# One diffusion block on one core: the loads of the beginning in another order, 1.4 MB of them cut or put off, c turned with the filter's vectors, the latents scaled by two engines, and context's tokens turned later

## The chip, the core and the metric

The kernel runs on one core of a Trainium2 chip, with these engines: TensorE (matrix products and transposes, into eight banks of PSUM), VectorE, ScalarE, GpSimd and SyncE, which here only issues loads. ScalarE and GpSimd issue loads too. Weights lie in HBM. The metric is the device time of one execution in microseconds (us); lower is better. All times in this text are microseconds unless they say otherwise, and "at 52.10" means 52.10 us after the start of the profiled span.

## The reference, cut to what matters

One block works on 512 latent tokens `x` and 256 context tokens `ctx` of width 1024 in float32. The beginning, which the change touches, is:

```python
x = x + pos_embed_2d(rows, cols, D)                   # half of the width by row, half by column
mod   = silu(c)     @ w_mod + b_mod                   # shifts, scales, gates for latents
mod_c = silu(c_ctx) @ w_mod + b_mod                   # the same for context
h  = rmsnorm(x,  pre_norm1) * (1 + sc1)  + sh1
hc = rmsnorm(xc, pre_norm1) * (1 + csc1) + csh1
z  = h @ w_in                                         # 3088 columns
zc = hc @ w_in[:, HY_COLS:]                           # context: only the mLSTM columns, gates among them
# the hyena filter: a small network of positions, times a decay
h = sin(freq * (zf @ w1 + b1)); h = sin(freq * (h @ w2 + b2)); h = sin(freq * (h @ w3 + b3))
filter = (h @ w4) * exp(-t * abs(deltas))             # then its spectrum
```

Behind it come the long convolution (by spectra), the mLSTM in both directions, the output projection, a router, and 16 experts of three matrices of 8 MB each, 404 MB in all, each used once. The last part is most of the time.

## The kernel before

All is written out by hand: each engine runs its own list, and the lists meet in semaphores (`wait_ge` on one side, `then_inc` on the other). A load increments its semaphore by 16 when it has landed. SyncE issues nearly all loads, in the order written, and its loads land in about that order.

**Weights.** A ring of eight slots of 2 MB takes the tiles of `LOADS`: four tiles of w_mod, here m0 to m3 (`mod_tile(0)` to `mod_tile(3)` use them), then six of w_in, i0 to i5, two of w_out, then the experts'. m0 and m2 share slot 0, m1 and m3 slot 1, i0 slot 0 again; a tile that reuses a slot is issued once the products of the tile before it there are done (`S["p_w"]`). The other two thirds of w_mod, in sixteen parts of 1 MB, are multiplied by the vector on VectorE (`row_parts`), between its convolutions (`conv`).

**The beginning, engine by engine.** TensorE turns the small vectors (L569 and L586 to L588), runs the filter's three layers (L582), each waiting for the sine before it, makes eight taps of the filter (L597), which VectorE multiplies by the decays `dcy` (L1533), and then `mod_tile(0)` and `mod_tile(1)` (L616), spectra 0 to 2 of the filter (L665), `mod_tile(2)`, spectrum 3, `mod_tile(3)`. The products with w_mod take silu(c) and silu(c_ctx) as `cpad`. ScalarE makes the decays (L1252), the sines (L1255), copies the first half of each spectrum (L1263), and squares the six tiles of tokens, context's two first (L1275); the square root of the sums (L1287) follows. VectorE adds the positions to x (L1551), makes parts of each spectrum (L1557, L1558), and after the reciprocal (L1566) normalizes context's and the latents' tiles (L1571); it copies the rows of w_mod's products to `mrow` (L1581).

**Turning.** TensorE turns `mrow` (`mod_turn`, L636), from which VectorE works out scale and shift (`aff1`, six small operations), and turns the normalized tokens, one k of eight at a time, latents and context in turn (L696). ScalarE scales and shifts the eight of the latents (L1293) and VectorE the eight of context (L1618), into `ht`. Then come the gates (L706), for all tokens, and tile 0 of w_in (`hyena_tile(0)`, L716): four groups m of eight products, 6.9 us each.

```python
            pe.wait_ge(S["a_htl"], KD)
            pe.wait_ge(S["v_htc"], KD)
            pe.wait_ge(d_gate, 32)
```

Of the kernel before, what the change touches and what calls it, by code (L numbers as in the profile page):

```python
# [51 lines left out]


def shape_constants():
# [17 lines left out]
    def emb(n):  # L72
# [4 lines left out]
    pe = np.concatenate([np.broadcast_to(er[:, None, :], (rows, GRID_W, D // 2)),  # L77
                         np.broadcast_to(ec[None, :, :], (rows, GRID_W, D // 2))], axis=-1)
    pe = np.ascontiguousarray(pe.reshape(L, D).astype(np.float32))
# [8 lines left out]
    dl = np.ascontiguousarray(np.broadcast_to(deltas[None, :], (P, HY)).astype(np.float32))  # L88
# [11 lines left out]
    return {"cst": cst, "pos": pe, "zft": zft, "dl": dl, "dft": tiles(fwd), "idft": tiles(inv)}  # L100
# [14 lines left out]
def block_kernel(nc, A, out):  # L115
    ctx = ExitStack()
    with ctx:
# [241 lines left out]
        def _(sp):  # L359

            def rows(dst, r, src, n):
                sp.dma_start(dst[r:r + n, :], src.rearrange("(a b) -> a b", b=P)).then_inc(d_vec2, 16)
# [133 lines left out]
        def _(pool):  # L496
            g = nc.gpsimd
            g.memset(vr2, 0.0).then_inc(S["g_ms"], 1)
# [4 lines left out]
            for r, n, src in ((R_C, 8, A["c"][0]), (R_CC, 8, A["c_ctx"]), (R_PRE1, 8, A["pre_norm1"][0]),  # L503
# [49 lines left out]
        def _(pe):  # L553
# [13 lines left out]
            pe.wait_ge(d_cst, 32)  # L567
            pe.wait_ge(d_vec2, 16 * N_VEC2)
            tr(B[1][:, 0:R2_ROWS], vr2[0:R2_ROWS, :], upper(R2_ROWS)).then_inc(S["p_vt"], 1)  # L569

            for n in range(3):
                if n < 2:
                    pe.wait_ge(*((d_filt, 32), (d_fw, 64))[n])
                if n:
                    pe.wait_ge(S["a_fil"], n)
                for half in range(2):
                    r = slice(FH * half, FH * (half + 1))
                    if n == 0:
                        w, src = fw1[0:FEMB, :], zft[0:FEMB, half * LC:(half + 1) * LC]
                    else:  # L580
                        w, src = (fw2, fw3)[n - 1][r, :], fh[r, :]
                    x = mm(B[2][r, (n % 2) * LC:(n % 2 + 1) * LC], w, src, start=True, stop=True)  # L582
                x.then_inc(S["p_fil"], 1)
                if n == 0:
                    pe.wait_ge(d_vec1, 16 * N_VEC1)
                    tr(B[0][:, 0:R1_ROWS], vr1[0:R1_ROWS, :], upper(R1_ROWS))  # L586
                    tr(B[0][:, 128:140], vr3[0:12, 0:2 * P:2], upper(12))
                    tr(B[0][:, 140:152], vr3[0:12, 1:2 * P:2], upper(12)).then_inc(S["p_vt"], 1)  # L588
            users[0] = users[1] = (S["v_vt"], 2)
            pe.wait_ge(S["v_fws"], 2)  # L590
            pe.wait_ge(S["a_fil"], 3)
            for n, (w, c) in enumerate(TAPS):
                b = 4 + n % 4
                r = slice(FH * (c // 2), FH * (c // 2 + 1))
                if n >= 4:
                    pe.wait_ge(S["v_kf"], n - 3)
                mm(B[b][:, :], fh[r, (c % 2) * P:(c % 2 + 1) * P], fws[r, w, :], start=True, stop=True)\  # L597
                    .then_inc(S["p_kf"], 1)
                users[b] = (S["v_kf"], n + 1)
# [8 lines left out]
            def mod_tile(i):  # L608
# [3 lines left out]
                if kp == 0:  # L612
                    take(2)
# [1496 lines left out]
```

## Time and profile before

| what | value |
|---|---|
| median of three runs | 1329.31 (1327.12 to 1329.52) |
| the profiled execution | 1328.1, span 1326.1 |
| TensorE busy | 1206.1 (91%) |
| VectorE, ScalarE, GpSimd busy | 351.3 (26%), 187.8 (14%), 30.6 (2%) |
| moved from HBM | 453 MB, mean 343 GB/s over the span |
| granted clock of TensorE | 0.996 of full speed |

The profiled execution's time is 2.0 more than its span: what lies around the span. Busy shares are means over the whole; the stages differ, so the page is read by stretches, and the waits by what ended last.

### The profile page before, as it was taken

How to read it: one execution, taken by the hardware profiler on the slowest of the kernel's cores; microseconds unless marked ns; L12 is line 12 of the kernel's file. 1: busy time of each engine (PE TensorE's matmuls, PEld its weight loads, DVE VectorE, ACT ScalarE, POOL GpSimd, SP SyncE). 2: the span in 40 equal slices, each digit the busy share in tenths (PEclk: the TensorE clock that was granted, in tenths of full speed). 3: DMA queues.
4: the chain of work that ended last, by engine and by line, in shares of the span. 5: the costliest groups of instructions: out<-in, count | busy, mean ns of one | idle time of the engine just before them, and what ended most of it. 6: DMA issues, size and time to landing. Idle time of an engine off the chain costs nothing.

```text
span 1326.1 us, 12939 instructions
## 1 busy us (share of the span) xinstructions
PE 1206.1 (91%) x5274; PEld 505.1 (38%) x5274; DVE 351.3 (26%) x625; ACT 187.8 (14%) x388; POOL 30.6 (2%) x56
## 2 busy tenths in 40 slices
PE   5999999999999999998989798888979898897996
PEld 1444454554554353342325234232423422242332
DVE  3775739444450110210201111020102102010213
ACT  2510020133310111010101001010200101010012
POOL 2000020000000001000000000000000000000000
PEclk9999999999999999999999999999999999999998
DMA  9965410306168999999999999999999999999994
GB/s 347 400 233 207 143 64 0 128 1 254 66 250 363 415 426 428 427 428 429 428 428 428 429 428 428 428 428 430 428 428 428 428 429 428 429 429 427 428 427 166
DMA packets 44776, 455.55 MB, mean 344 GB/s; under 512 B 6192, under 2 KB 6304, under 8 KB 16970
## 3 DMA queue, kind: packets, MB, share of 16 engines
q1 hardware_dynamic: 44098, 454.94, 82.1%
q8 instruction: 22, 0.36, 0.1%
q10 hardware_dynamic: 264, 0.11, 0.0%
q0 software_dynamic: 384, 0.07, 0.0%
q14 instruction: 8, 0.07, 0.0%
HBM read 453.01 MB, written 2.10 MB: 343 GB/s over the span
## 4 chain that ended last, share of the span: by engine, by line
PE 60%; DMA 33%; DVE 4%; issue 1%; ACT 1%; SPq 1%; DVEq 0%; ACTq 0%
DMA ring<-in_w_exp_up 28%; PE B L1151 15%; PE B L1120 11%; PE B L716 6%; PE B L953 4%; PE B L1062 4%; PE B L837 3%; DMA ring<-in_w_exp_down 3%; PE B L895 2%; DMA ring<-in_pos 2%; PE B L1212 2%; PE B L766 2%; DVE moe L2029 1%; PE B L1133 1%; DVE yacc L2020 1%
## 5 line engine op out<-in xcount | busy, mean ns | idle before, releaser
L1120 PE MATMUL B<-ring,moe 128*64 128x512 f32 x2032 | 454.9, 596 | 75.9 <-DMA ring<-in_w_exp_up 41.9
L1120 PEld LDWEIGHTS B<-ring,moe 128*64 128x64 f32 x2032 | 139.4, 137 | 384.8 <-issue 247.0
L2029 DVE TENSOR_TENSOR moe<-moe,B 64x512 f32<-64x512 f32 x64 | 43.8, 685 | 699.5 <-PE B L1120 698.2
L1151 PE MATMUL B<-ring,moe 128*64 128x512 f32 x1008 | 221.2, 594 | 4.5 <-DMA ring<-in_w_exp_down 4.4
L1151 PEld LDWEIGHTS B<-ring,moe 128*64 128x64 f32 x1008 | 71.2, 137 | 142.8 <-issue 138.0
L1438 ACT ACTIVATE moe<-B 64x512 f32<-64x512 f32 x64 | 37.9, 592 | 413.8 <-PE B L1120 412.6
L716 PE MATMUL B<-ring 128*128 128x512 f32 x192 | 83.6, 594 | 0.0
L1212 PE MATMUL B<-moe 128*128 128x512 f32 x112 | 56.7, 618 | 4.5 <-DVE yacc L2020 4.1
L1062 PE MATMUL B<-moe,xl 128*128 128x128 f32 x448 | 55.0, 281 | 0.0
L1448 ACT ACTIVATE moe<-B 64x512 f32<-64x512 f32 x31 | 18.4, 592 | 251.3 <-PE B L1151 250.9
L1062 PEld LDWEIGHTS B<-moe,xl 128*128 128x128 f32 x448 | 53.9, 196 | 0.0
L716 PEld LDWEIGHTS B<-ring 128*128 128x128 f32 x192 | 36.1, 190 | 45.1 <-issue 45.1
L837 PE MATMUL B<-ring 128*128 128x512 f32 x96 | 43.3, 592 | 0.0
L2020 DVE TENSOR_TENSOR yacc<-yacc,B 128x512 f32<-128x512 f32 x56 | 38.3, 684 | 10.8 <-PE B L1212 10.4
L895 PE MATMUL B<-ring 128*128 128x512 f32 x64 | 33.1, 614 | 0.0
L1212 PEld LDWEIGHTS B<-moe 128*128 128x128 f32 x112 | 18.4, 189 | 37.7 <-DVE yacc L2020 26.8
L953 PE MATMUL B<-ring 128*128 128x512 f32 x64 | 28.5, 592 | 0.0
L953 PE MATMUL B<-ring,fr 128*128 128x512 f32 x64 | 28.3, 595 | 0.0
L766 PE MATMUL B<-ring 128*128 128x512 f32 x64 | 27.9, 594 | 0.0
L837 PEld LDWEIGHTS B<-ring 128*128 128x128 f32 x96 | 17.4, 190 | 17.7 <-issue 17.7
L1133 PEld LDWEIGHTS B<-cst_sb,moe 128*128 128x128 f32 x128 | 18.9, 204 | 11.5 <-issue 8.2
L2033 DVE COPY moe<-B 128x512 f32<-128x512 f32 x16 | 11.1, 692 | 44.2 <-PE B L1133 44.2
(335 smaller groups left out, 800.7 us busy)
## 6 DMA issues: line engine op xcount, KB each, us to landing
ring<-in_w_exp_up SPq DMA_DIRECT2D x64, 2048.0 KB, 31.8
ring<-in_w_exp_gate SPq DMA_DIRECT2D x63, 2048.0 KB, 30.4
ring<-in_w_exp_down SPq DMA_DIRECT2D x63, 2048.0 KB, 34.0
ring<-in_w_in SPq DMA_DIRECT2D x6, 2048.0 KB, 9.0
ring<-in_w_mod SPq DMA_DIRECT2D x10, 1024.0 KB, 7.6
ring<-in_w_mod SPq DMA_DIRECT2D x4, 2048.0 KB, 14.2
fr<-in_w_mod SPq DMA_DIRECT2D x6, 1024.0 KB, 9.3
ring<-in_w_out SPq DMA_DIRECT2D x2, 2048.0 KB, 8.4
```

Source lines behind the costliest of these rows:

```text
L716: x = mm(B[b][:, :], w[:, k, m * P:(m + 1) * P], ht[:, k, LC:], start=(k == 0), stop=(k == KD - 1))
L766: x = mm(B[b][:, :], w[:, k, m * P:(m + 1) * P], ht[:, k, LC:], start=(k == 0), stop=(k == KD - 1))
L837: x = mm(B[b][:, :], ht[:, k, t * P:(t + 1) * P], w[:, k, :], start=(k == 0), stop=(k == KD - 1))
L895: x = mm(B[O_BANK[c]][:, :], ht[:, k, LC + c * P:LC + (c + 1) * P], wo_in[:, k, :], start=(k == 0), stop=(k == KD - 1))
L953: x = mm(B[b][:, :], lhs, wo[half][:, k, :], start=(k == 0), stop=(k == KD - 1))
L1062: x = mm(B[6 + g][:, k * P:(k + 1) * P], x3[:, c, pair_rows(dk)], psel[:, c, :], start=(c == 0), stop=(c == NLT - 1))
L1120: x = mm(B[n][rows, :], xst[:, 2 * q + k, CAP * e2:CAP * (e2 + 1)], w[:, k, n * CH:(n + 1) * CH], start=(q == 0 and k == 0), stop=(q == 3 ...
L1151: x = mm(B[bank][CAP * half:CAP * (half + 1), :], src[:, q // 2, k * P + at:k * P + at + CAP], wd[:, k, half * CH:(half + 1) * CH], start= ...
L1212: mm(B[6 + half][:, :], pwt[:, c, :], ye[:, half * CH:(half + 1) * CH], start=True, stop=True).then_inc(S["p_sca"], 1)
L1438: a.activation(sil[o, n // 2, :], B[n][i, :], ACT.Silu).then_inc(S["a_sil"], 1)
L2020: v.tensor_tensor(dst, dst, B[6 + half][:, :], ALU.add).then_inc(S["v_yacc"], 1)
L2029: v.tensor_tensor(hid[o, n // 2, :], sil[o, n // 2, :], B[n][o, :], ALU.mult).then_inc(S["v_hid"], 1)
```

## The change

- **SyncE's order.** c and c_ctx come first, now with the filter's vectors in `vr2`; then the part of the constants that is needed early (260 of 836 columns), the filter's inputs and weights, m0, x, the positions, the transform `dft`, m1, ctx, m2, m3, then the rest of the constants. conv_w, conv_b and ml_norm go to GpSimd's queue; zft, filt_w1 and filt_w2 go from ScalarE's queue to SyncE's. The wait for a memset of `vr2` is gone with the memset.
- **Fewer bytes.** Instead of a table of 2 MB the positions are `pcol` (128 x 512, added to all four tiles) and `prow` (8 x 512), read by two loads that each repeat rows over 64 partitions. The decay rates come as one row of 2 KB, which TensorE spreads over 128 partitions by a product with ones.
- **c.** silu(c) is now c / (1 + exp(-c)), by one exponential and three small operations of VectorE, between layers 0 and 1 of the filter. The other vectors are turned after the sixth tap.
- **Decays.** ScalarE makes them after the third sine, from PSUM.
- **Tokens.** x is squared and normalized before ctx. TensorE turns three k of the latents, then `mrow`, then the other five; ScalarE scales the even k and VectorE the odd. Context's eight k are turned within tile 0, behind its first group, and the gates are behind its second.

```diff
-            sp.dma_start(cst[:, :], A["cst"]).then_inc(d_cst, 16)
-            sp.dma_start(dlb, A["dl"]).then_inc(d_cst, 16)
-            sp.wait_ge(S["g_ms"], 1)
+            for r, src in ((R_C, A["c"][0]), (R_CC, A["c_ctx"])):
+                sp.dma_start(vr2[r:r + 8, :], src.rearrange("(a b) -> a b", b=P)).then_inc(d_vec2, 16)
+            sp.dma_start(cst[:, 0:C_EARLY], A["cst"][:, 0:C_EARLY]).then_inc(d_cst, 16)
+            sp.dma_start(zft[0:FEMB, :], A["zft"]).then_inc(d_filt, 16)
+            sp.dma_start(fw1[0:FEMB, :], A["filt_w1"][0]).then_inc(d_filt, 16)
+            sp.dma_start(dlr[0:1, :], A["dl"]).then_inc(d_filt, 16)
...
             for n in range(len(LOADS)):
+                if n == 1:
+                    sp.dma_start(x3, A["x"][0].rearrange("(c p) n -> p c n", p=P)).then_inc(d_x, 16)
+                    sp.dma_start(xn[:, 0, CH:D], A["pcol"]).then_inc(d_pos, 16)
+                    for r in range(2):
+                        sp.dma_start(xn[FH * r:FH * (r + 1), :, 0:CH],
+                                     A["prow"].rearrange("(c r) n -> r c n", r=2)[r].partition_broadcast(FH)).then_inc(d_pos, 16)
+                    sp.dma_start(slot(5, 0, 2048), A["dft"]).then_inc(d_dft, 16)
                 if n == 2:
                     sp.dma_start(cx, A["ctx"][0].rearrange("(c p) n -> p c n", p=P)).then_inc(d_ctx, 16)
-                    sp.dma_start(x3, A["x"][0].rearrange("(c p) n -> p c n", p=P)).then_inc(d_x, 16)
-                    sp.dma_start(xn, A["pos"].rearrange("(c p) n -> p c n", p=P)).then_inc(d_pos, 16)
                 if n == 4:
+                    sp.dma_start(cst[:, C_EARLY:C_COLS], A["cst"][:, C_EARLY:C_COLS]).then_inc(d_gate, 16)
...
+            pe.wait_ge(d_filt, 48)
+            filter_layer(0)
+            mm(B[3][:, :], cst[0:1, C_ONE:C_ONE + P], dlr[0:1, :], start=True, stop=True).then_inc(S["p_vt"], 1)
...
+            pe.wait_ge(S["v_xn"], NTT)
+            for k in range(3):
+                rows_of_latents(k)
             mod_turn(0, 1)
+            for k in range(3, KD):
+                rows_of_latents(k)
...
+                    if m == 0 and i == 0:
+                        for c in range(KD):
+                            rows_of_context(c)
+                    if m == 1 and i == 0:
+                        gates()
...
+            act.wait_ge(S["p_vt"], 2)
+            for c in range(NLT):
+                a.activation(dcy[:, c, :], B[3][:, :], ACT.Exp, scale=cst[:, C_TC + c:C_TC + c + 1]).then_inc(S["a_dec"], 1)
...
+            filter_odd(2)
+            act.wait_ge(d_ctx, 16)
+            squares(4)
+            squares(5)
```

SyncE's queue, before the change, from the program's start to i0 (`ring<-in_w_mod` with no wait are m0 and m1):

```order
L363 DMA cst_sb<-in_cst 128x836
L364 DMA ring<-in_dl 128x512
...
L375 DMA ring<-in_dft 128x2048
L391 DMA ring<-in_w_mod 128x2x2048 x2
L435 DMA moe<-in_ctx 128x2x1024
L436 DMA xl<-in_x 128x4x1024
L437 DMA ring<-in_pos 128x4x1024
L391 DMA ring<-in_w_mod 128x2x2048 [waits p_w] x2
...
L441 DMA col<-in_ml_gate_b 128x16
L391 DMA ring<-in_w_in 128x8x512 [waits p_w]
```

and of the changed kernel (the rows left out between its first two are the other small loads, and in the end the gates' columns and bias):

```order
L362 DMA ring<-in_c 8x128
...
L363 DMA cst_sb<-in_cst 128x260
...
L389 DMA ring<-in_w_mod 128x2x2048
L433 DMA xl<-in_x 128x4x1024
L434 DMA ring<-in_pcol 128x512
L436 DMA ring<-in_prow 64x4x512 x2
L438 DMA ring<-in_dft 128x2048
L389 DMA ring<-in_w_mod 128x2x2048
L440 DMA moe<-in_ctx 128x2x1024
L389 DMA ring<-in_w_mod 128x2x2048 [waits p_w] x2
L442 DMA cst_sb<-in_cst 128x576
...
L389 DMA ring<-in_w_in 128x8x512 [waits p_w]
```

x, the positions and the transform now stand between m0 and m1; the positions are three loads, and the late constants have come between m3 and i0.

ScalarE, before, from its first computation to the copy of spectrum 2's first half (L1252 are the decays, L1255 the sines, L1263 copies of a spectrum's first half, L1275 squares):

```order
L1252 ACTIVATE ring<-ring,cst_sb 128x512 [waits d_cst]
L1252 ACTIVATE ring<-ring,cst_sb 128x512 x3
L1255 ACT_TABLE_LOAD
L1255 ACTIVATE ring<-ring 128x256 [waits v_arg] x3
L1258 ACT_TABLE_LOAD
L1258 ACTIVATE col<-col 128x16 [waits v_vt]
L1263 ACTIVATE ring<-B 128x512 [waits p_ksp]
L1275 ACTIVATE ring,col<-moe 128x1024 [waits d_ctx]
L1275 ACTIVATE ring,col<-moe 128x1024 [waits a_ss]
L1263 ACTIVATE ring<-B 128x512 [waits p_ksp]
L1275 ACTIVATE ring,col<-xl 128x1024 [waits a_ss,v_x] x4
L1263 ACTIVATE ring<-B 128x512 [waits p_ksp]
```

and of the changed kernel over the same stretch (L1289 the sines, L1292 the decays, L1297 the copies, L1309 squares; `moe` holds ctx):

```order
L1286 ACTIVATE col<-col 128x16 [waits v_vt]
L1289 ACT_TABLE_LOAD
L1289 ACTIVATE ring<-ring 128x256 [waits v_arg] x3
L1292 ACT_TABLE_LOAD
L1292 ACTIVATE ring<-B,cst_sb 128x512 [waits p_vt]
L1292 ACTIVATE ring<-B,cst_sb 128x512 x3
L1297 ACTIVATE ring<-B 128x512 [waits p_ksp]
...
L1297 ACTIVATE ring<-B 128x512 [waits p_ksp]
L1309 ACTIVATE ring,col<-xl 128x1024 [waits a_ss,v_x] x2
L1297 ACTIVATE ring<-B 128x512 [waits p_ksp]
L1309 ACTIVATE ring,col<-moe 128x1024 [waits a_ss,d_ctx]
L1309 ACTIVATE ring,col<-moe 128x1024 [waits a_ss]
```

The decays have moved from ahead of the sines to behind them, with a load of the table between, and context's squares have moved behind the copy of spectrum 2.

## Rows read from the trace of the kernel before

**Rows 1.** Stretch of the program: length, busy us of each engine, clock, load share, GB/s
```profile
434.00:1326.00 892.00, 794.94 (x3700) 301.43 (x3696) 123.11 (x210) 95.62 (x175) 13.87 (x22) 1.00 0.98 418
```

**Rows 2.** Chain that ended last, to 460 us: start us, us, what
```profile
9.39 25.93 DMA ring<-in_pos
...
52.10 5.47 ACT ring L1293 x8
57.62 3.64 PE B L706 x48
61.26 27.66 PE B L716 x64
```

**Rows 3.** Timeline of TensorE, 8 to 50 us: start us, us, instructions [idle before]
```profile
8.65 1.12 PE L582 MATMUL B<-ring 33*64 33x256 f32 x4
12.12 0.40 PE L586 MATMUL B<-cst_sb,ring 80*128 80x80 f32 x1 [2.35 <-DMA ring<-in_b_mod]
...
12.79 1.12 PE L582 MATMUL B<-ring 64*64 64x256 f32 x4
...
26.85 3.64 PE L616 MATMUL B<-ring,moe 128*32 128x512 f32 x32 [0.37 <-DVE moe L1545]
30.42 10.57 PE L665 MATMUL B<-yacc,ring 128*128 128x512 f32 x24
41.55 1.92 PE L616 MATMUL B<-ring,moe 128*32 128x512 f32 x16 [0.56 <-DMA ring<-in_w_mod]
```

**Rows 4.** Timeline of ScalarE, 0 to 45 us
```profile
7.01 2.56 ACT L1252 ACTIVATE ring<-ring,cst_sb 128x512 f32<-128x512 f32 x4
...
11.26 0.42 ACT L1255 ACTIVATE ring<-ring 128x256 f32<-128x256 f32 x1 [0.39 <-DVE ring L1517]
...
18.32 0.42 ACT L1255 ACTIVATE ring<-ring 128x256 f32<-128x256 f32 x1 [2.58 <-DVE ring L1517]
18.76 1.28 ACT L1258 ACT_TABLE_LOAD   x1
...
40.40 1.06 ACT L1275 ACTIVATE ring<-xl 128x1024 f32<-128x1024 f32 x1
...
41.46 0.58 ACT L1263 ACTIVATE ring<-B 128x512 f32<-128x512 f32 x1
```

**Rows 5.** Timeline of VectorE, 8 to 53 us
```profile
21.04 1.29 DVE L1533 TENSOR_TENSOR yacc<-B,ring 128x512 f32<-128x512 f32 x2 [2.74 <-PE B L597]
...
24.63 1.87 DVE L1533 TENSOR_TENSOR yacc<-B,ring 128x512 f32<-128x512 f32 x3
...
43.94 0.18 DVE L1566 RECIPROCAL col<-col 128x6 f32<-128x6 f32 x1
...
49.46 0.68 DVE L1581 COPY fr<-B 128x512 f32<-128x512 f32 x1
...
52.10 0.99 DVE L1618 TENSOR_SCALAR ring<-B,col 128x256 f32<-128x256 f32 x2
```

**Rows 6.** Loads: two stretches, issues on SyncE, issue to landing of x and of one load alone
```profile
6.00:9.00 3.00, 0.60 (x3) 0.47 (x5) 0.22 (x1) 2.99 (x5) 2.64 (x5) 1.00 1.07 233
10.00:20.00 10.00, 4.02 (x15) 1.73 (x17) 5.47 (x14) 3.37 (x5) 0.00 (x0) 1.00 1.01 415
...
0.75 0.40 SPq L363 DMA_DIRECT2D cst_sb<-in_cst  x1
...
6.31 0.94 SPq L391 DMA_DIRECT2D ring<-in_w_mod  x2
...
xl<-in_x SPq DMA_DIRECT2D x1, 2048.0 KB, 22.4
...
L402 SPq DMA_DIRECT2D fr<-in_w_mod x1: 327/327/327, 75.5 to 75.5; - x1
...
DMA to landing us min/median/max: 4.9/4.9/4.9
```

**Rows 7.** Timeline of VectorE near 97 us
```profile
96.87 0.81 DVE L1640 TENSOR_SCALAR ring<-B,col 128x512 f32<-128x512 f32 x1 [2.90 <-PE B L716]
```

More of the change, by code:

```diff
@@ L76, in shape_constants @@
     er, ec = emb(rows), emb(GRID_W)
[L77 to L79 removed]
+    pcol = np.ascontiguousarray(np.tile(ec, (P // GRID_W, 1)).astype(np.float32))
+    prow = np.ascontiguousarray(er.astype(np.float32))
     w = 2.0 * np.pi * np.arange(L) / L
@@ L564, in upper @@
                 return ident[0:m, 0:m]
-            pe.wait_ge(d_cst, 32)
+            pe.wait_ge(d_cst, 16)
             pe.wait_ge(d_vec2, 16 * N_VEC2)
[L569 to L599, printed above, removed]
-            users[2] = users[3] = (S["a_fil"], 3)
+            tr(B[1][:, 0:R2_EARLY], vr2[0:R2_EARLY, :], upper(R2_EARLY)).then_inc(S["p_vt"], 1)
             def weights(kind, i):
@@ L680, in _ @@
             filter_spectrum(0)
+            mod_tile(1)
             pe.wait_ge(S["v_kf"], len(TAPS))
@@ new lines, in rows_of_context @@
+            def rows_of_context(k):
+                b = [n for n in range(3, 8) if n != hy_bank[0]][k % 4]
+                take(b)
+                htc_bank[k] = b
+                for c in range(NCT):
+                    x = tr(B[b][:, c * P:(c + 1) * P], cx[:, c, k * P:(k + 1) * P], idn)
+                x.then_inc(S["p_htc"], 1)
+                users[b] = (S["v_htc"], k + 1)
+            pe.wait_ge(S["v_xn"], NTT)
+            for k in range(3):
+                rows_of_latents(k)
+            mod_turn(0, 1)
@@ new lines, in _, with gates @@
+            for k in range(3, KD):
+                rows_of_latents(k)
+            def gates():
+                pe.wait_ge(S["v_htc"], KD)
+                pe.wait_ge(d_gate, 48)
+                take(0)
+                for k in range(KD):
+                    for n in range(3):
+                        x = mm(B[0][32 * n:32 * n + 16, 0:LC], wgate_sb[:, k, :], ht[:, k, n * LC:(n + 1) * LC],
+                               start=(k == 0), stop=(k == KD - 1))
+                x.then_inc(S["p_gt"], 1)
+                users[0] = (S["a_gt"], 3)
@@ L724, in hyena_tile @@
                         mod_row(1)
+            pe.wait_ge(S["a_htl"], KD // 2)
+            pe.wait_ge(S["v_htl"], KD // 2)
             hyena_tile(0)
@@ L1247, in link @@
                 act.wait_ge(S["a_ch"], done[0])
-            act.wait_ge(d_cst, 32)
-            for c in range(NLT):
-                a.activation(dcy[:, c, :], dlb, ACT.Exp, scale=cst[:, C_TC + c:C_TC + c + 1]).then_inc(S["a_dec"], 1)
+            act.wait_ge(S["v_ch"], 1)
+            a.activation(sd2[:, 0:1], idle[:, 0:1], ACT.Exp)
+            act.wait_ge(S["v_vt"], 1)
+            a.activation(mcur[:, 0:16], v2t[:, R_C:R_C + 16], ACT.Exp, scale=-1.0).then_inc(S["a_th"], 1)
             for n in range(3):
@@ L1281, in _ @@
             filter_odd(1)
-            for t in range(NCT, NTT):
-                squares(t)
+            squares(2)
+            squares(3)
             filter_odd(2)
+            act.wait_ge(d_ctx, 16)
+            squares(4)
+            squares(5)
             act.wait_ge(S["a_ss"], NTT)
@@ L1290, in _ @@
             act.wait_ge(S["v_kf"], len(TAPS))
-            for k in range(KD):
+            for k in range(0, KD, 2):
                 act.wait_ge(S["p_htl"], k + 1)
```

206 lines of the change are left out of this document (114 added, 92 removed).

## The prediction

> **What bounds the kernel now.** I read the stretches of the page first. From 434 us on the loads run at 418 GB/s and the loads' share is 0.98 [rows 1]: that part is bound by bytes, the change touches none of them, and each of its first loads is released by a step of TensorE before it. So only TensorE's arrival there can move the end. I then read the chain of waits from the start [rows 2]: 25.9 us are the load of the positions (landed 35.3), then additions, norms and turning on VectorE and ScalarE, then ScalarE scales the latents (52.10 to 57.57), TensorE makes the gates (57.62 to 61.26), and from 61.26 it multiplies without a hole: tile 0 of w_in with the 12 small transposes behind it, 27.66 us, ends at 88.92. The reader is to see that a microsecond taken before 88.92 is one off the end, if TensorE still finds its inputs afterwards. The profiled execution took 1328.1 (span 1326.1); the median of the runs is 1329.31, 1.2 above it. I sum against the profiled one and add the difference to that median. This kernel's measurement can tell about 0.2%, 2.7 us.
>
> **The filter comes earlier.** Layer 0 starts at 8.65, after the small vectors have landed; layer 1 starts at 12.79 although its sine ended at 11.68, since the vectors' transposes stand ahead of it with a wait of 2.35 us for b_mod [rows 3, 4]. After the change the queue of ScalarE begins with its four small vectors, 1.3 us earlier than now, c and c_ctx are SyncE's first, and b_mod's wait stands behind six taps. I take 6.3 for layer 0 (bounds 5.8 and 7.3). Third sine: now 18.32, 9.67 after layer 0, of which 1.1 was the held layer; so 6.3 + 8.6 = 14.9. The three new operations for c on VectorE are of 16 columns and lie in its waits between layers.
>
> But the decays move behind the sines. Now they are over at 9.57, in nobody's way; afterwards they need 0.44 for the sine, 1.28 for the table and 2.56 for four activations [rows 4], and VectorE's first tap waits for all four: 14.9 + 4.3 = 19.2, against 21.04 [rows 5]. The 3.4 us of the filter have become 1.8. The last taps follow 4 us behind (three products, two operations on row 0, one product: rows from 21.04 to 25.3 less a 0.25 wait), so mod_tile(0) starts at 19.2 + 4.7 = 23.9 instead of 26.85 [rows 3, 5]. The page "ScalarE: Activation LUTs" of the Trainium skill, section "What ACT_TABLE_LOAD costs", adds a drain of about 1.38 us to each load of a table. The trace does not show one: the sine ends at 18.74, the load starts at 18.76, takes 1.28, and the next activation starts at 20.05 [rows 4]. By the page's figure the tap would come at 20.6; the wait for the next load, below, would swallow that.
>
> **The loads.** Before x has landed the old order moves about 9.9 MB: constants, the filter's, the transform (1.0), m0 and m1 (2.1 each), ctx (1.0), x (2.1); x lands 22.4 after its issue, and the rate is 415 GB/s [rows 6]. The new order is 0.95 MB of small loads, m0, x, positions (0.26 + 1.05), transform, m1, ctx, m2, m3. There are 13 small loads ahead of m0 instead of 11; at 0.5 us each (11 from 0.75 to 6.31 [rows 6]) m0 is issued at 7.4 instead of 6.3, with far fewer bytes ahead of it. A load of 1 MB alone took 4.9 to land [rows 6], 2.5 of it bytes, so 2.4 are fixed: m0 lands at 7.4 + 2.4 + 5.1 = 14.9, x at 20.0. The positions: 0.26 MB (0.6), and two loads of prow, each 0.52 MB into 64 partitions. No row prices those alone. Lower bound 2.5 us for the two, the rate of [rows 6]. Upper bound 5.6: the two halves of filt_w4, also 64 partitions each, are 0.52 MB and are the main bytes issued from 4.1 to 5.4; the stretch 6 to 9 us, with the loads' share at 1.07, moved 233 GB/s [rows 6]; the first part of that stretch slower still. I take 4.5 (1.05 MB at 233), because it is the one row with such loads, although that stretch holds other small loads too. Then the positions are in at 25.1, the transform at 27.7, m1 at 32.8, ctx 35.3, m2 40.4, m3 45.5.
>
> The page "SBUF — State Buffer" of the Trainium skill, section "Door 1: The DMA port swizzle (why [64,N] ≈ [32,N])", says that 64 partitions reach half of the ports and gives 196 GB/s for a load of 1 MiB there. By it the two prow loads would take 5.4 us as an estimate and m1 would land 0.9 later than in my sum. The trace agrees as far as 233 GB/s goes, but it cannot tell the shape from the time of day.
>
> **TensorE from there.** mod_tile(0) 23.9 to 25.8; the first spectrum takes 3.52 (three take 10.57 [rows 3]) and waits for the transform: 27.7 to 31.2. mod_tile(1) stands behind it and waits for m1 until 32.8, ends at 34.7; this is the stall that is late next. Spectra 1 and 2 to 41.7; mod_tile(2), 1.92 [rows 3], to 43.6; spectrum 3 to 47.1; mod_tile(3) to 49.0, m3 in time.
>
> ScalarE copies spectrum 2's first half when it ends, 40.0 to 40.6, and only then squares ctx twice, at 40.6 and 41.8 (1.06 and the reading of the sum). From the start of the last square (40.40) to the reciprocal (43.94) is 3.54 now, 0.58 of it a copy that then comes ahead of the squares [rows 4, 5]; so the reciprocal is at 41.8 + 2.95 = 44.8, 0.85 later than now. x plus positions becomes 8 additions of half the width, about 0.65 each as the products of that width [rows 5]; they lie between 27 and 35, where VectorE waits for two spectra, and cost nothing unless the positions land later than 29. The six norms and spectrum 3's parts are the same work, so the copy of mrow goes from 49.46 to 50.3 [rows 5]; mod_tile(3) has ended by then.
>
> From that copy to VectorE's first scaling is 2.64 now (49.46 to 52.10). Then VectorE scales four latents at 0.81 (the row of that shape [rows 7]), 3.2; ScalarE's four are done sooner, since it may start after three of the six operations. So tile 0 can start at 50.3 + 2.64 + 3.2 + 0.05 = 56.2, 5.1 earlier than now. Its weights i0 are issued at 43.6 and their bytes come behind m3 (45.5) and 0.4 MB of constants and gates: 51.6.
>
> Into tile 0 come the gates, 3.64 [rows 2], and context's transposes. Those were hidden behind ScalarE's scaling. Now TensorE does 16 of them in between, in four banks, and the fifth waits for VectorE's first scaling (0.54, row of 52.10 [rows 5]): lower bound 1.8 us, upper 4.3 (eight scalings); with four of them ahead of the eighth pair 2.7. So 56.2 + 27.66 + 3.64 + 2.7 = 90.2 against 88.92: **1.3 us later**. Splitting the scaling gains 2.2 us of VectorE and ScalarE and shows 2.7 of transposes: nearly nothing is left of it.
>
> **Behind tile 0.** VectorE's sums of w_mod start some 9 us later and so do the loads released by them; VectorE has 2.90 us of idle time before 96.87, waiting for TensorE [rows 7]. With its operations of tile 0 put one behind another from the new start it is done at about 95.5, while TensorE's next result comes at 98.0: it has caught up there, and all that follows is as now. Without that cover the sums would hold up mod_row(1), 7 us later still. So span 1327.4, profiled time 1329.4, median 1329.31 + 1.3 = **1330.6**.
>
> **Rivals.**
> (1) The prow loads run at the full rate. m1 lands at 30.8, every step from mod_tile(1) on is 2.0 earlier: tile 0 ends at 88.2, 0.7 early, **1328.6**. For it: the loads of w_in with 2 KB rows run near full rate. Against: 233 GB/s at 6 to 9 us.
> (2) The bytes show fully. The small loads are issued faster than now, m0 starts by 6.3, m1 lands by 28.5, and mod_tile(1) never waits. TensorE then goes on from 25.8 without a hole; spectrum 2 ends at 38.3 instead of 41.7, tile 0 at 86.8, with context's transposes at their lower bound 85.9, with layer 0 at its bound as well 85.4: 2.1 to 3.5 early, **1326.3** near its far end. Against: 13 issues at 0.5 us.
> (3) The other side: m1 lands at 35 or later, since reading 16 KB 64 times over, or half the lanes, costs more than the upper bound, or the queue runs dry at 5 to 8 us where it is not dry now. It becomes slower by over 2.7 us when m1 lands past 34.2, that is 1.4 beyond my sum: at 35.3 the end is 3.8 later, **1333.1**.
> (4) The change does not do what it says, since tile 0 waits for i0 (issued after mod_tile(2), behind three more small loads): it would have to land 6 us later than in my sum to cost 1.4; then as (3).
>
> **How the numbers follow.** Forecast 0.40; (1) 0.22; (2) 0.22; (3) with (4) 0.16. The forecast's own range, by its bounds (prow at most 5.6, transposes 1.8 to 4.3, and prow not under 3.5, or it is rival (1)): 1328.7 to 1333.3. The whole range is 1326.3 to 1332.9; it leaves out some 0.07 of (2) and 0.1 of (3), (4) and the forecast's end. Faster by over 0.2% needs under 1326.65: three quarters of (2) and a little of (1), 0.19. Slower by over 0.2% is above 1331.97: (3), (4) and a tenth of the forecast, 0.20. Within: 0.61.
>
> **What the profile would show.** Layer 0 at 6.3, third sine at 14.9, first tap at 19.2 behind the fourth decay. mod_tile(1) waiting for in_w_mod after spectrum 0, and the load of prow landing at about 25: at 23 it is rival (1). The reciprocal at 44.8, tile 0's first product at 56.2, its last at 90.2. A wait of VectorE for TensorE near 98. I am wrong if mod_tile(1) does not wait, or if TensorE has holes after tile 0.

## The result

Median 1333.97 against 1328.97 before (6 executions each, 1331.64 to 1336.21 and 1327.12 to 1329.52): ratio 1.0037 [1.0027, 1.0047], slower by 0.4%. A later group of five executions of the same kernel gave 1335.16, ratio 1.0042 [1.0028, 1.0056]. The prediction, 1330.6 with a range to 1332.9, was too low by 3.4, and the median lies 1.1 above its range. The profiled execution took 1331.64, span 1329.6; it is the fastest of its six.

The timeline of TensorE after the change (start, us, line, instructions, idle before), where [rows 3] stood before; L590 is `mod_tile`, L639 a spectrum, L747 tile 0, L718 context's transposes, L736 the gates, L771 the 12 small transposes at the end of tile 0:

```profile
23.58 1.93 PE L590 MATMUL B<-ring,moe 128*32 128x512 f32 x16
29.82 5.21 PE L639 MATMUL B<-yacc,ring 128*128 128x512 f32 x8 [4.32 <-DMA ring<-in_dft]
34.96 1.92 PE L590 MATMUL B<-ring,moe 128*32 128x512 f32 x16
36.81 7.13 PE L639 MATMUL B<-yacc,ring 128*128 128x512 f32 x16
43.88 1.92 PE L590 MATMUL B<-ring,moe 128*32 128x512 f32 x16
...
57.84 2.38 PE L747 MATMUL B<-ring 128*128 128x512 f32 x5 [1.11 <-ACT ring L1329]
...
64.78 2.82 PE L718 MATMUL B<-cst_sb,moe 128*128 128x128 f32 x16
68.06 7.13 PE L747 MATMUL B<-ring 128*128 128x512 f32 x16 [0.47 <-DVE ring L1668]
75.12 3.64 PE L736 MATMUL B<-ring,moe 128*16 128x256 f32 x48
78.69 14.00 PE L747 MATMUL B<-ring 128*128 128x512 f32 x32
92.63 0.92 PE L771 MATMUL B<-cst_sb,moe 16*128 16x16 f32 x12
```

The reader is to see one hole: 4.32 us, waiting for the transform. It stands ahead of spectrum 0, not of `mod_tile(1)`, and it is followed by a spectrum of 5.21 us where the next two take 7.13 together. The end of tile 0 has moved from 88.85 to 92.63, by 3.8; the span has grown by 3.5. I use this one mark, the start of the 12 small transposes, for all kernels below. What the span holds behind the mark is not quite constant (1236.4 to 1239.2 over the fourteen profiles), so a difference of 1 us at the mark of two executions need not be one in their times.

Stretches of the same trace (length; PE, PEld, DVE, ACT, POOL busy; clock, load share, GB/s), beside [rows 6]:

```profile
6.00:9.00 3.00, 2.95 (x8) 0.68 (x6) 2.05 (x8) 1.92 (x3) 2.92 (x6) 1.00 0.54 136
9.00:12.00 3.00, 1.13 (x6) 0.30 (x7) 1.88 (x5) 0.42 (x1) 0.00 (x0) 1.00 1.05 296
...
20.00:22.00 2.00, 2.00 (x8) 1.07 (x8) 1.93 (x4) 0.00 (x0) 0.00 (x0) 1.00 1.05 345
22.00:24.00 2.00, 2.00 (x8) 0.45 (x10) 2.00 (x4) 0.00 (x0) 0.00 (x0) 1.00 1.06 215
24.00:26.00 2.00, 1.50 (x16) 0.26 (x8) 1.54 (x6) 0.00 (x0) 0.00 (x0) 1.00 1.17 244
26.00:28.00 2.00, 0.00 (x0) 0.00 (x0) 0.42 (x1) 0.00 (x0) 0.00 (x0) 1.00 0.94 314
28.00:30.00 2.00, 0.18 (x1) 0.18 (x2) 2.00 (x4) 0.00 (x0) 0.00 (x0) 0.87 0.99 414
30.00:33.00 3.00, 3.00 (x4) 1.33 (x5) 0.07 (x1) 0.00 (x0) 0.00 (x0) 0.52 1.03 429
```

Three things stand there. The queue is half empty at 6 to 9 us (136 GB/s, load share 0.54, where before it was 233 and 1.07). From 20 to 28 us the loads' share is full but the rate is 215 to 345: in that time land x (21.5), pcol (22.6) and the two loads of prow (24.9 and 27.5). And right behind the hole the granted clock is at the lower of its levels (0.52 from 30 to 33 us), which costs spectrum 0 about 1.5 of its 5.21 us against the 3.70 of spectrum 3.

SyncE's issues (L372 are the two halves of filt_w4), and below them, from the view of the loads up to 60 us, issue to landing:

```profile
6.06 1.24 SPq L372 DMA_DIRECT2D ring<-in_filt_w  x2
...
7.82 0.40 SPq L389 DMA_DIRECT2D ring<-in_w_mod  x1
8.27 0.46 SPq L433 DMA_DIRECT2D xl<-in_x  x1
8.77 0.50 SPq L434 DMA_DIRECT2D ring<-in_pcol  x1
9.31 1.49 SPq L436 DMA_DIRECT2D ring<-in_prow  x2
10.85 3.56 SPq L438 DMA_DIRECT2D ring<-in_dft  x1
14.45 1.48 SPq L389 DMA_DIRECT2D ring<-in_w_mod  x1
...
xl<-in_x SPq DMA_DIRECT2D x1, 2048.0 KB, 13.2
ring<-in_dft SPq DMA_DIRECT2D x1, 1024.0 KB, 18.9
```

x lands at 8.27 + 13.2 = 21.5, the transform at 10.85 + 18.9 = 29.8. Between them stand 2.4 MB (pcol, prow, transform), which at 415 GB/s would be 5.7 us and took 8.3.

### The profile page after: what moved, and what is told of

Its sections match the earlier page's. It is cut to its first block, busy times and chain, and to the rows that moved or that the text cites. A ratio compares the mean times of both kernels' runs of the same rounds, so it can differ in the third digit from the quotient of the medians.

```text
span 1329.6 us, 12956 instructions
## 1 busy us (share of the span) xinstructions
PE 1212.1 (91%) x5277; PEld 506.1 (38%) x5277; DVE 355.0 (27%) x636; ACT 184.8 (14%) x385; POOL 30.8 (2%) x56
## 4 chain that ended last, share of the span: by engine, by line
PE 61%; DMA 32%; DVE 4%; issue 1%; ACT 1%; SPq 1%; DVEq 0%; ACTq 0%
DMA ring<-in_w_exp_up 28%; PE B L1189 15%; PE B L1158 11%; PE B L747 6%; PE B L991 4%; PE B L1100 4%; PE B L875 3%; DMA ring<-in_w_exp_down 3%; PE B L933 2%; PE B L1250 2%; PE B L804 2%; DMA ring<-in_dft 1%; DVE moe L2079 1%; PE B L1171 1%; DVE yacc L2070 1%
## 5 line engine op out<-in xcount | busy, mean ns | idle before, releaser
L747 PE MATMUL B<-ring 128*128 128x512 f32 x192 | 84.1, 595 | 1.6 <-ACT ring L1329 1.1
L747 PEld LDWEIGHTS B<-ring 128*128 128x128 f32 x192 | 35.9, 190 | 46.2 <-issue 44.2
L991 PE MATMUL B<-ring,fr 128*128 128x512 f32 x64 | 28.3, 595 | 0.0
L804 PE MATMUL B<-ring 128*128 128x512 f32 x64 | 27.9, 594 | 0.0
L1171 PEld LDWEIGHTS B<-cst_sb,moe 128*128 128x128 f32 x128 | 18.9, 204 | 11.5 <-issue 8.2
L2083 DVE COPY moe<-B 128x512 f32<-128x512 f32 x16 | 11.1, 692 | 44.8 <-PE B L1171 44.8
```

What stands on the lines that cost most here:

```text
L747: x = mm(B[b][:, :], w[:, k, m * P:(m + 1) * P], ht[:, k, LC:], start=(k == 0), stop=(k == KD - 1))
L804: x = mm(B[b][:, :], w[:, k, m * P:(m + 1) * P], ht[:, k, LC:], start=(k == 0), stop=(k == KD - 1))
L991: x = mm(B[b][:, :], lhs, wo[half][:, k, :], start=(k == 0), stop=(k == KD - 1))
```

## The experiments

Twelve runs: eleven edits, and the changed kernel once more. "End" is the start of the 12 small transposes in the profiled execution.

| kernel | built on | median | ratio to before, 95% | x, dft landed | end |
|---|---|---|---|---|---|
| before | | 1328.97 | | 30.2, 12.6 | 88.85 |
| the changed kernel | | 1333.97 | 1.0037 [1.0027, 1.0047] | 21.5, 29.8 | 92.63 |
| c1_again | changed, no edit | 1335.16 | 1.0042 [1.0028, 1.0056] | 22.9, 31.5 | 94.53 |
| e1_wide | changed | 1330.96 | 1.0014 [1.0006, 1.0023] | 22.2, 28.1 | 90.71 |
| e2_halves | changed | 1335.69 | 1.0050 [1.0037, 1.0063] | 21.3, 29.6 | 92.23 |
| e3_order | changed | 1336.10 | 1.0047 [1.0033, 1.0061] | 31.1, 19.6 | 97.04 |
| e4_busy | changed | 1334.66 | 1.0042 [1.0028, 1.0056] | 24.8, 33.0 | 95.73 |
| e5_turn | e1_wide | 1329.89 | 1.0003 [0.9994, 1.0012] |  22.5, 28.4 | 89.46 |
| e6_queues | e1_wide | 1333.47 | 1.0039 [1.0025, 1.0053] |  19.7, 25.5 | 93.87 |
| e7_bytes | before | 1328.69 | 0.9997 [0.9988, 1.0006] |  30.8, 12.9 | 89.79 |
| e8_fill | e5_turn | 1329.98 | 1.0005 [0.9996, 1.0014] |  22.3, 28.1 | 90.77 |
| e9_m1_behind | e5_turn | 1328.08 | 0.9990 [0.9981, 0.9999] | 22.3, 28.1 | 87.85 |
| e10_both | e8 and e9 | 1330.23 | 1.0006 [0.9997, 1.0015] |  22.1, 27.9 | 90.22 |
| e11_squares | e9_m1_behind | 1327.82 | 0.9986 [0.9977, 0.9995] |  22.5, 28.3 | 87.25 |

The kernel before ran beside each group, at medians from 1328.83 to 1329.57, so kernels of different groups are compared by their ratios.

**e1_wide and e2_halves: is it the width of the positions' loads, or the repeated rows?** Both read prow from a table of 1 MB in which the rows are already repeated; e1 by one load to 128 partitions, e2 by two to 64 each.

```diff
-                    for r in range(2):
-                        sp.dma_start(xn[FH * r:FH * (r + 1), :, 0:CH],
-                                     A["prow"].rearrange("(c r) n -> r c n", r=2)[r].partition_broadcast(FH)).then_inc(d_pos, 16)
+                    sp.dma_start(xn[:, :, 0:CH], A["prow"]).then_inc(d_pos, 16)      # e1
+                    for r in range(2):                                               # e2
+                        sp.dma_start(xn[FH * r:FH * (r + 1), :, 0:CH], A["prow"][FH * r:FH * (r + 1)]).then_inc(d_pos, 16)
```

> The changed kernel, with the row half of the positions as a table of 1 MB that one load brings into all 128 partitions, the same bytes into the same places. Theory (width): the two loads of prow are slow because each reaches 64 partitions; the positions then land some 2.3 us earlier (25.2 instead of 27.5), the transform at 27.5 instead of 29.8, TensorE waits some 2 us for it instead of 4.3, and tile 0 of w_in ends 2 us earlier, 4 us if the clock no longer falls: span 1325.5 to 1327.7 against 1329.6. Rival (order): the two loads cost nothing much and the transform is late through its place behind x: then its landing moves by under 0.5 us and the time not at all.

> As the kernel with the wide table, but the table of 1 MB comes in two loads of 64 partitions each; no row of HBM is read twice. Theory (width): as slow as in the changed kernel, 2 KB packets at about 159 ns, positions at 27.5, span as the changed kernel's (1329.6). Rival (repeated rows): the slowness comes from reading 2 KB rows 64 times over; then it is as fast as the wide load, positions at 25.2, span 2 us or more below.

The stretches from 22 to 26 us of e1_wide, then of e2_halves:

```profile
22.00:24.00 2.00, 2.00 (x4) 0.57 (x3) 1.85 (x4) 0.00 (x0) 0.00 (x0) 0.50 1.10 414
24.00:26.00 2.00, 2.00 (x9) 0.40 (x12) 1.77 (x7) 0.00 (x0) 0.00 (x0) 0.50 1.02 415
```

```profile
22.00:24.00 2.00, 2.00 (x6) 1.02 (x5) 1.99 (x4) 0.00 (x0) 0.00 (x0) 0.50 1.05 215
24.00:26.00 2.00, 2.00 (x11) 0.40 (x12) 1.69 (x4) 0.00 (x0) 0.00 (x0) 0.50 1.15 236
```

At equal load share the one load runs at 414 GB/s and the two at 215 to 236. Between the landings of x and of the transform lie 5.9 us in e1_wide, 8.3 in e2_halves and in the changed kernel, so the table without repeated reads is no better: **the width is the cost**, 2.4 us between the landings. That two loads stand where one stood was not tried apart from the width, but the load share is full while the rate is halved, and m0 and x, also two loads, one behind the other, land 5.2 apart (16.3 and 21.5), at 403 GB/s. In the times the cost is larger: 4.7 between the medians of e1 and e2, which differ in nothing else, and by the ratios 3.1 to 3.7 between e1 and the changed kernel. Why it is more than 2.4 is not shown. In e1_wide the end came 1.9 earlier, as expected, but the span (1328.6) stayed above the expected 1325.5 to 1327.7, and the kernel is still slower than the one before. The page "SBUF — State Buffer" of the Trainium skill, section "Door 1: The DMA port swizzle (why [64,N] ≈ [32,N])", gives 64 partitions half of the ports; the roughly halved rate here agrees with it.

**c1_again: how far does one execution stand for the next?** No edit.

> The changed kernel once more, nothing edited, beside the others of this group: it tells how far one execution's loads stand for the next. Theory: the late transform is in every execution, landing at 29 to 33 us (29.8 in the first profile), TensorE waits 4 us or more for it, and the median is again 1333.5 to 1335. Rival: the first set of times was of one chip or one hour, and the median now is under 1332.

In this execution x landed 1.4 later (8.26 + 14.6) with the same issues, and all behind it followed: the transform at 31.5, the end at 94.53. The order of events is the same; the size of the loss depends on when the first large loads land. x landed between 21.3 and 24.8 in ten profiles of kernels with the same queue up to x. TensorE waited 3.38 for the transform, not 4 or more, as `mod_tile(0)` took 3.64 here at the lower clock.

**e3_order: the transform and m1 ahead of x and the positions.** The two loads moved in SyncE's list, nothing else (in short form):

```diff
                 if n == 1:
-                    (x, pcol, prow)
                     sp.dma_start(slot(5, 0, 2048), A["dft"]).then_inc(d_dft, 16)
                 if n == 2:
+                    (x, pcol, prow)
                     sp.dma_start(cx, ...)
```

> The changed kernel with the transform and m1 ahead of x and the positions. Theory (TensorE's hole and the clock): the transform lands by 19, m1 by 24, TensorE goes through to spectrum 2 without a wait and at the full clock (spectrum 0 in 3.5 us instead of 5.2), but the positions land at about 34.7, the last square comes after them, reciprocal at 45.7 instead of 46.7, and tile 0 ends 1 us earlier: span 1328.6. Rival (the hole alone sets it): with the hole of 4.3 us and the clock's 1.7 us gone the end comes 6 us earlier, 1323.6.

Both figures were missed: the span was 1334.7. TensorE runs through from 24.9 to 40.8, but VectorE waits 11.7 us for prow, which landed at 38.7 and not at 34.7, and the reciprocal came at 50.59 instead of 46.72; from there to the copy of mrow VectorE has no wait. `mod_tile(2)` waits for m2, whose bytes stand behind x and both slow loads, as they did before this edit, and which was issued 2.8 later (28.36), since `mod_tile(0)`, whose slot it takes, ended later:

```profile
28.00:32.00 4.00, 4.00 (x16) 1.59 (x16) 0.00 (x0) 0.60 (x1) 0.00 (x0) 1.00 1.09 203
32.00:36.00 4.00, 4.00 (x22) 1.37 (x16) 0.00 (x0) 0.00 (x0) 0.00 (x0) 1.00 1.05 230
...
45.95 3.64 PE L590 MATMUL B<-ring,moe 128*32 128x512 f32 x16 [5.12 <-DMA ring<-in_w_mod]
49.52 4.79 PE L639 MATMUL B<-yacc,ring 128*128 128x512 f32 x8
```

The slow stretch (8 us at 203 to 230 GB/s) went along with prow, wherever it stood. `mod_tile(2)` at 3.64 instead of 1.92 is again the lower clock behind a hole (0.50 from 46 to 50 us).

**e4_busy: does the clock's fall behind the hole cost the time?** Nine products that nobody reads stand ahead of the wait for the transform.

```diff
+            take(3)
+            for _ in range(9):
+                mm(B[3][:, 0:256], idn, cst[:, 0:256], start=True, stop=True)
             pe.wait_ge(d_dft, 16)
```

> The changed kernel with nine products of 128x256 that nobody reads on TensorE ahead of its wait for the transform, 3.9 us of work in the hole of 4.3. Theory (clock): the granted clock does not fall, spectrum 0 takes 3.5 us instead of 5.2 after the same landing at 29.8; mod_tile(1) then waits for m1 (34.7) for 1.3 us, so only about 0.3 us of the 1.7 come through before mod_tile(1), and the span falls by 0.3 to 1.5. Rival (clock is nothing of it, other executions vary for another reason): spectrum 0 stays at 5.2 us, no difference, and the executions scatter over 4 us as the changed kernel's do.

In its profile spectrum 0 took 3.70, at the full clock, but x landed at 24.8 and the transform at 33.0 there, and the median is within 0.7 of the two of the unedited kernel: no gain. `mod_tile(1)` waited 1.31 for m1 behind the faster spectrum. What the clock gives there, the wait for m1 takes.

**e5_turn: the turning alone.** In e1_wide, the turning as before the change.

```diff
-            for k in range(3):
-                rows_of_latents(k)
             mod_turn(0, 1)
-            for k in range(3, KD):
-                rows_of_latents(k)
+            for k in range(KD):
+                rows_of_latents(k)
+                rows_of_context(k)
...
-            pe.wait_ge(S["a_htl"], KD // 2)
-            pe.wait_ge(S["v_htl"], KD // 2)
+            pe.wait_ge(S["a_htl"], KD)
+            gates()
             hyena_tile(0)
```

> e1_wide, and in it the tokens turned as in the kernel before: mrow first, then latents and context by turns, ScalarE scales all eight latents, the gates ahead of tile 0. It prices the splitting alone. Theory: the splitting loses, since from the copy of mrow to the end of tile 0 it is 40.37 us in the changed kernel and 39.46 in the one before; so tile 0 ends 0.9 earlier than in e1_wide's profile (90.71), at 89.8, and the median falls from 1330.96 to 1330.1. Rival: the splitting gains 5 us of start and hides most of the transposes, and the 0.9 is from elsewhere (the clock): then the median is 1331.0 or more.

As expected: 1329.89. From the copy of mrow (50.67) to the mark it is 38.79, against 40.36 in e1_wide (50.35 to 90.71): splitting the scaling and putting context into tile 0 costs 1.6 between these marks, and 1.1 by the medians or 1.5 by the ratios, whose intervals just overlap. With the wide load and the old turning the changed kernel is level with the one before (1.0003), so these two account for its loss.

**e6_queues: m0 issued earlier.** In e1_wide, four small loads of the filter go to ScalarE's queue, so that m0 is issued at 5.28 instead of 7.80.

```diff
-                sp.dma_start(fw2[FH * half:FH * (half + 1), :], A["filt_w2"][0]).then_inc(d_fw, 16)
+                act.dma_start(fw2[FH * half:FH * (half + 1), :], A["filt_w2"][0]).then_inc(d_fw, 16)
...                                                                     (fw3 likewise)
```

> e1_wide, and in it the four loads of filt_w2 and filt_w3 are issued by ScalarE behind its four vectors, so that SyncE reaches m0 four issues (2 us) sooner. Theory: the queue starts its large loads late, each lands 2 us earlier than in e1_wide, mod_tile(1) no longer waits (1.23 there), tile 0 ends at 89.5, the median is 1329.7. Rival A: four more issues on ScalarE hold up the filter, layer 1 comes later than 8.3 us and nothing is gained (1331.0). Rival B: the loads land 2 us earlier, but the stretch at half clock between 22 and 28 us stays and is what counts, so that only some 0.5 is gained (1330.5).

2.5 slower (3.3 by the ratios), in the direction of rival A and beyond it, and for another reason: ScalarE's first sine comes at 9.34, some 1.1 later, but layer 1 waits until 14.01 for its weights. Their loads now run beside filt_w4's halves and m0:

```profile
ring<-in_filt_w ACTq DMA_DIRECT2D x4, 16.0 KB, 6.4
...
14.01 1.12 PE L647 MATMUL B<-ring 64*64 64x256 f32 x4 [5.00 <-DMA ring<-in_filt_w]
```

From issue to landing they take 6.4 us instead of 2.2 in e1_wide, and layer 1 starts at 14.01 instead of 8.72. The large loads did come 2.5 earlier (x at 19.7), and no tile of w_mod was waited for, but `mod_tile(0)` started at 30.01 instead of 24.39. The late start of m0 was the price of the filter's early one.

**e7_bytes: fewer bytes in the kernel before.** pcol and the wide prow instead of the table of 2 MB, all else as before.

> The kernel before, with one edit: the positions as a table of 0.26 MB and one of 1.05 MB, each one load to 128 partitions, instead of one of 2.1 MB, and eight additions of half the width. It takes the idea of fewer bytes alone, and at full width. Theory: the positions end the longest wait of the kernel before (landed 35.3), land 1.9 us earlier (0.79 MB at 415 GB/s), and the reciprocal moves until spectrum 2 holds it: by 0.6 to 1.9, I take 1.0, so 1328.0. Rival: TensorE and ScalarE hold the reciprocal anyway, and the time stays within 0.3 of 1328.9.

1328.69 against 1329.12: the rival holds. 0.79 MB fewer brought 0.4, which is not clear of noise; the interval reaches from 1.6 faster to 0.8 slower. (Its end of 89.79 comes from an execution in which the clock was at 0.50 from 27 to 30 us and `mod_tile(0)` and `(1)` took 5.34 instead of 3.64.)

**e8_fill, e9_m1_behind, e10_both: the clock at 22 to 28 us, and the order around m1.** In e1_wide, e2_halves, e4_busy, c1_again and e5_turn the clock was at 0.50 there. e8 fills the holes between the filter's layers; e9 moves `mod_tile(1)`; e10 does both.

```diff
             filter_layer(1)
+            for _ in range(6):                                                       # e8, behind layer 2 too
+                mm(B[2][:, 0:256], idn, cst[:, 0:256], start=True, stop=True)
...
             filter_spectrum(0)
-            mod_tile(1)
             pe.wait_ge(S["v_kf"], len(TAPS))
             filter_spectrum(1)
+            mod_tile(1)                                                              # e9
             filter_spectrum(2)
```

> e5_turn (wide positions, tokens turned as before), and in it six products of 128x256 (0.25 us each) that nobody reads, behind layer 1 and six behind layer 2 of the filter, where TensorE waits 1.9 and 2.0 us for a sine. Theory: these holes are what the clock answers to between 22 and 28 us (0.50 there in e5_turn); filled, the clock is 1.00, mod_tile(0) takes 1.92 instead of 3.64, spectrum 0 starts at 25.3 instead of 28.4; but mod_tile(1) still waits for m1 until about 33, so that the median falls by 0.5 at most, to 1329.4. Rival: the fall has nothing to do with these holes (the execution e6_queues had one of 5 us and no fall), and mod_tile(0) still takes 3.64, the median stays at 1329.9.

> e5_turn, and in it mod_tile(1) stands behind spectrum 1 instead of ahead of it. Theory: its wait for m1 (1.06 in e5_turn) is gone, since spectrum 1 fills the time until m1 has landed; the reciprocal comes 1.1 earlier (44.0), tile 0 too, the median is 1328.8. Rival: m3 is issued 3.6 later, since it waits for mod_tile(1), and mod_tile(3) then waits for it: as much is given back, 1329.9 or more.

> e8_fill and e9_m1_behind together. Theory: with the clock at 1.00 spectra 0 and 1 are over at 32.4 and m1 lands at 33, so that spectrum 2 ends at 38.6 instead of 42.3; then m2 and m3 bind, mod_tile(3) ends at 48 and the copy of mrow comes at 48 instead of 50.7: up to 2.6 earlier than e5_turn, 1327.3, which would be faster than the kernel before. Rival A (the fill does nothing): as e9_m1_behind. Rival B: the loads set the time of m3 (45.5 at the earliest), and the gain is 1 at most, 1328.9.

The timeline of e8_fill:

```profile
9.28 1.12 PE L651 MATMUL B<-ring 64*64 64x256 f32 x4
10.32 4.77 PE L673 MATMUL B<-cst_sb 128*128 128x256 f32 x12
15.03 0.65 PE L651 MATMUL B<-ring 64*64 64x256 f32 x4
15.61 2.86 PE L677 MATMUL B<-cst_sb 128*128 128x256 f32 x12
...
27.24 3.64 PE L589 MATMUL B<-ring,moe 128*32 128x512 f32 x16
```

The fill did not prevent the fall: `mod_tile(0)` still took 3.64. And it did not fit its holes: the first six products (12 in the row) took 4.77 and the second 2.86 where I had counted 1.5, so that layer 2 came at 15.03 instead of 12.02. So the fall comes without these holes too. The test is not clean, as the late taps opened another hole (1.64 ahead of 22.02, 0.65 in e5_turn). `mod_tile(0)` came 2.5 later than in e5_turn, `mod_tile(1)` only 1.3 later, since its wait for m1 (1.06 in e5_turn) was used up; the mark is 1.3 later, and yet the median stayed at 1329.98. In e10_both no such wait is left to cover the lateness: the mark is 2.4 later than in e9_m1_behind, and the median 2.2 higher in the same group. 1330.23 misses the theory (1327.3) and both rivals, as none of them gave the fill a price.

In e9_m1_behind TensorE waits for no load from `mod_tile(0)` on but 0.24 us for m3:

```profile
28.12 7.13 PE L638 MATMUL B<-yacc,ring 128*128 128x512 f32 x16
35.18 1.92 PE L589 MATMUL B<-ring,moe 128*32 128x512 f32 x16
...
46.47 1.92 PE L589 MATMUL B<-ring,moe 128*32 128x512 f32 x16 [0.24 <-DMA ring<-in_w_mod]
```

The reciprocal came at 43.52 (44.0 expected), the end at 87.85, and the median fell by 1.8 (1.7 by the ratios) instead of 1.1. It is the first of these kernels whose whole interval lies below the one before. In its profile the reciprocal is 1.6 earlier than in e5_turn: 1.06 are the wait for m1, the rest comes from products that ran faster. The granted clock was at 1.00 from 20 to 30 us, and still `mod_tile(0)` took 3.03, not 1.92.

**e11_squares: context's squares ahead of the copy of spectrum 2.** In e9_m1_behind, `squares(4)` and `squares(5)` stand before `filter_odd(2)`.

> e9_m1_behind, and in it ScalarE squares context's two tiles ahead of the copy of spectrum 2's first half, not behind it: in e9_m1_behind it waits 2.16 us for that spectrum while ctx has landed. Theory: the squares fill that wait, the reciprocal moves from 43.5 to 42.2 (there VectorE's parts of spectrum 2 hold it), and the copy of mrow from 49.05 to 48.4, where mod_tile(3) holds it; so 0.65 earlier, median 1327.4, faster than the kernel before by 0.1 to 0.15%. Rival: m3 lands later than 46.4 in most executions, mod_tile(3) and not the reciprocal sets the copy of mrow, and the median stays within 0.3 of 1328.1.

```profile
42.40 0.18 DVE L1604 RECIPROCAL col<-col 128x6 f32<-128x6 f32 x1
...
48.43 0.69 DVE L1619 COPY fr<-B 128x512 f32<-128x512 f32 x1 [0.42 <-PE B L589]
```

The reciprocal moved by 1.1, the copy of mrow by 0.6, and that copy now waits for `mod_tile(3)`, as expected. The time does not show it: the median is 0.26 below that of e9_m1_behind, within the 0.3 that the rival gave, and the intervals of the two ratios overlap almost whole. m3 was not late in this profile, so the rival's reason is not seen either. Moving the squares is thus not shown to gain. The ratio is 0.9986 [0.9977, 0.9995]: faster than both kernels, by some 1.9 us against the one before and 7 against the changed one (by its ratio of 1.0037 to 1.0042).

## Why the prediction was wrong

**The step that failed** is the timeline of the loads, and in it above all "m0 lands at 7.4 + 2.4 + 5.1 = 14.9, x at 20.0". m0 landed at 16.3 (7.82 and 8.5 from issue to landing) and x at 21.5 in the profile, m0 at 16.7 and x at 22.9 in c1_again. From m0 to x it is 5.2, as in the sum, so in the profile the whole error lies in m0. 0.4 of it is the issue: the six loads to 64 partitions among the small ones took 0.6 to 0.7 us each, not 0.5. The other 1.0 is the time from issue to landing, 8.5 instead of 7.5. The sum took that from a load that was alone, with "far fewer bytes ahead of it"; but the halves of filt_w4, 0.52 MB to 64 partitions, are issued from 6.06 to 7.30, right ahead of m0, and from 9 to 12 us the rate is 296 GB/s at a full load share. That term was put at nothing. How much of the 1.0 is theirs no run shows; in the other profiles with this queue m0 took 8.3 to 9.5. For x the error is 1.3 to 4.8 over the ten profiles.

The loads alone would not have left the range: m1 at 34.7 is 1.9 later than in the sum, and 1330.6 + 1.9 is 1332.5. Tile 0 (+0.5 in all from the copy of mrow on) and the median (+1.1), both below, brought the time past 1332.9.

**Right mechanism, term a little small: prow.** I took 4.5 us for the two loads, with a bound of 5.6. x to transform took 8.3 instead of the 7.7 of my sum, so prow cost about 5.1 (4.9 from pcol's landing to its own), 2.4 more than the one wide load of e1_wide. Both terms together put the transform at 29.8 (27.7 predicted) and m1 at 34.7 (14.45 and 20.3 from issue to landing; 32.8 predicted). Rival (3) drew the line at 34.2, and that rival is what happened: it gave 1333.1 for m1 at 35.3. Of its reasons it was the queue that ran half dry (load share 0.54 at 6 to 9 us), not a cost of prow above the upper bound.

**The place of the stall.** "mod_tile(1) ... waits for m1; this is the stall that is late next" did not show: the hole of 4.32 stands one step earlier, at the transform, and `mod_tile(1)` found m1 there. My sum had both waits (1.9 and 1.6), so the place of the second is wrong and the total, 3.5 against 4.3, not far off: `mod_tile(1)` ended 2.1 later than predicted, as the transform landed 2.1 later. The prediction's own sign of being wrong, that `mod_tile(1)` does not wait, came true. The fall of the clock behind the hole was not in the sum; spectrum 0 took 1.5 us longer, but at full clock TensorE would have waited for m1 until 34.7, so that it cost 0.3 in this execution.

**The sum, term by term, in the profile.** Reciprocal 46.72 instead of 44.8, +1.9, all from the above. From there to the copy of mrow 5.5, as predicted. To the start of tile 0 5.6 instead of 5.9. Tile 0 with gates and context 34.8 instead of 34.0: the transposes with their waits took 3.3 (64.78 to 68.06) instead of 2.7, within the bounds. Together +2.4: 92.63 instead of 90.2.

**The median.** I added 1.2, what the median stood above the profile before. After, it stands 2.3 above, since this profile was the fastest of its kernel; c1_again's execution, whose x landed at 22.9, is nearer the middle. That is 1.1 of the 3.4, and which execution is profiled is luck. The eleven executions of the changed kernel spread over 4.6 (1331.64 to 1336.21), those of e1_wide over 2.9. The range was too narrow, as it let the time of the first large loads vary by nothing.

**What held.** The filter, a little earlier throughout: layer 0 at 5.68 (6.3 predicted, and just below the bound of 5.8), third sine 14.37 (14.9), first tap 18.55 behind the fourth decay (19.2), `mod_tile(0)` 23.58 (23.9). The third sine ends at 14.79 and the load of the table starts at 14.80 and takes 1.28, the next activation starts at 16.10: the drain that the page "ScalarE: Activation LUTs" of the Trainium skill, section "What ACT_TABLE_LOAD costs", adds is again not there. And the split turning brought nothing, as forecast (2.2 gained against 2.7 shown, 0.5 lost); e5_turn prices it at 1.1 to 1.6 lost. VectorE's wait for TensorE near 98 is there (2.90, until 100.65). Behind tile 0 all is as before, only later: +3.8 at the mark, +3.5 in the span.

**What stays open.** What sets the clock's falls near 22 to 30 us: the same kernel had one at 22 to 28 and one at 32 to 36 in c1_again, and only one from 29 in the first profile; filling the holes of the filter did not end them. Why x lands at 21.3 in one execution and 24.8 in another behind the same issues. And the changed kernel's own idea, c with the filter's vectors and the decays behind the sines, was never put into the kernel before by itself, so what it is worth in time is not known.

## What to carry to other kernels

Count the partitions of a load as well as its bytes: a cut from 2.1 to 1.3 MB brought 0.4 us, not clear of noise, at full width where it was tried alone, and bringing the rows' half of the table by two loads to 64 partitions cost 3 to 5 us more than by one load to 128. When a load becomes the bound, ask what work that needs neither it nor anything late could stand ahead of its wait; moving one tile behind one spectrum gave 1.7 to 1.8 us, more than the fewer bytes were seen to give. And look at where two chains meet: in e6_queues the loads came 2.5 us earlier and the filter 5.6 later, and the later one decided.

## What the runs showed that I had not expected

- Small loads on a queue of their own are no shelter from large ones: 16 KB loads took 6.4 us instead of 2.2 when ScalarE issued them and SyncE issued filt_w4's halves and m0 some 2.5 us earlier (e6_queues).
- With the granted clock at 1.00, the same four products took 1.12 us (layers 1 and 2 of the changed kernel) and 0.65 once the six filling products had run ahead of them (e8_fill). In the same way `mod_tile(0)` took 3.03 in e9_m1_behind and 1.93 in the changed kernel's first profile, both at 1.00. So in these stretches that column does not tell how fast TensorE is; what else decides is open.
- A kernel that still waits for a load behind the slow stretch is less sensitive to the clock: in e1_wide and e5_turn `mod_tile(0)` ran at half the clock, 1.7 us longer, and without that TensorE would have waited as much longer for m1.
